# MLP up projection by Strassen's scheme: seven half-size products for a pair of chunks, with the down projection following pair by pair

## The reference, cut to what matters

```python
x = x + merged @ w_out[l]
h2 = rms_norm(x, norm2[l])
x = x + jnp.square(jax.nn.relu(h2 @ w_up[l])) @ w_down[l]     # w_up 1024 x 4096, w_down 4096 x 1024
return rms_norm(x, final_norm)
```

## Time and profile before

| what | us |
|---|---|
| median of three runs (2026.22, 2026.28, 2030.49) | 2026.28 |
| the profiled execution | 2030.5 |
| its span, first to last instruction | 2028.7 |
| PE busy | 1977.2 (97%) |
| DVE / ACT / POOL busy | 750.2 / 588.9 / 735.8 |
| granted TensorE clock, mean of the span | 0.993 |

### The profile page before, as it was taken

One profiled execution on the slowest core, in us unless ns is written; L12 is line 12 of the kernel. 1 busy time (PEld: TensorE's weight loads), 2 busy tenths in 40 slices (PEclk: granted clock), 3 DMA queues, 4 the chain that ended last, 5 costly groups with the idle time before them and its releaser, 6 DMA issues.

```text
span 2028.7 us, 28162 instructions
## 1 busy us (share of the span) xinstructions
PE 1977.2 (97%) x9984; PEld 1663.9 (82%) x9984; DVE 750.2 (37%) x1406; ACT 588.9 (29%) x1036; POOL 735.8 (36%) x633
## 2 busy tenths in 40 slices
PE   7999999999999999999999999999999999999998
PEld 6778887788888888888888887878888888888887
DVE  5535554667554544454421234321112112111222
ACT  5025544646444544455300011121011001101222
POOL 3442227623122212211344444434444444444441
PEclk9999999999999999999999999999999999999999
DMA  4311013331111011100111113111111111111112
GB/s 125 105 43 31 27 38 89 83 122 40 40 40 47 22 48 47 43 22 21 37 47 47 51 47 129 47 42 52 47 47 52 47 47 52 47 47 52 47 47 98
DMA packets 178293, 109.52 MB, mean 54 GB/s; under 512 B 11784, under 2 KB 171024, under 8 KB 178208
## 3 DMA queue, kind: packets, MB, share of 16 engines
q1 hardware_dynamic: 165984, 89.67, 15.6%
q10 hardware_dynamic: 12224, 18.70, 2.9%
HBM read 99.91 MB, written 11.59 MB: 55 GB/s over the span
## 4 chain that ended last, share of the span: by engine, by line
PE 89%; DVE 6%; issue 2%; ACT 2%; DMA 1%; SPq 0%; DVEq 0%; ACTq 0%
PE ps L582 23%; PE ps L583 23%; PE ps L584 23%; PE ps L702 6%; PE ps L691 3%; PE ps L677 2%; PE ps L672 1%; PE ps L624 1%; PE ps L626 1%; PE ps L625 1%; DVE tmp L1328 1%; DVE h_lo L1258 1%; DVE sumsq L1273 1%; PE ps L603 1%; PE ps L641 0%
## 5 line engine op out<-in xcount | busy, mean ns | idle before, releaser
L513 POOL TENSOR_TENSOR w_hi<-raw,ones 128x512 fp32r<-128x512 f32 x274 | 295.0, 1077 | 1207.9 <-PE ps L584 1192.1
L582 PE MATMUL ps<-h_hi,w_hi 128*128 128x512 f32 x1536 | 606.4, 395 | 11.8 <-DVE tmp L1328 3.4
L583 PE MATMUL ps<-h_lo,w_hi 128*128 128x512 f32 x1536 | 600.0, 391 | 0.0
L584 PE MATMUL ps<-h_hi,w_lo 128*128 128x512 f32 x1536 | 599.4, 390 | 0.0
L517 POOL TENSOR_TENSOR w_lo<-raw,w_hi 128x512 fp32r<-128x512 f32 x274 | 366.3, 1337 | 21.5
L582 PEld LDWEIGHTS ps<-h_hi,w_hi 128*128 128x128 f32 x1536 | 289.5, 188 | 69.6 <-DVE tmp L1328 5.9
L584 PEld LDWEIGHTS ps<-h_hi,w_lo 128*128 128x128 f32 x1536 | 288.9, 188 | 61.9
L583 PEld LDWEIGHTS ps<-h_lo,w_hi 128*128 128x128 f32 x1536 | 289.6, 189 | 54.5 <-issue 0.7
L582 PE MATMUL ps<-u_hi,w_hi 128*128 128x512 f32 x512 | 200.0, 391 | 2.7 <-DVE relu L1764 2.7
L584 PE MATMUL ps<-u_hi,w_lo 128*128 128x512 f32 x512 | 199.7, 390 | 0.0
L583 PE MATMUL ps<-u_lo,w_hi 128*128 128x512 f32 x512 | 199.6, 390 | 0.0
(11 more groups left out here) (232 smaller groups left out, 2378.9 us busy)
## 6 DMA issues: line engine op xcount, KB each, us to landing
raw<-in_w_in SPq DMA_DIRECT2D x116, 256.0 KB, 2.9
raw<-in_w_up SPq DMA_DIRECT2D x64, 256.0 KB, 2.7
raw<-in_w_down SPq DMA_DIRECT2D x64, 256.0 KB, 2.8
raw<-in_w_out SPq DMA_DIRECT2D x32, 256.0 KB, 2.8
x_in<-in_x SPq DMA_DIRECT2D x8, 512.0 KB, 7.7
raw_b<-in_w_out SPq DMA_DIRECT2D x16, 256.0 KB, 2.8
x_store<-X ACTq DMA_DIRECT2D x8, 512.0 KB, 2.8
bias_fox<-c_rows ACTq DMA_DIRECT2D x8, 512.0 KB, 4.5
```

The source lines that it names most:

```text
L513: pool.tensor_tensor(w_hi[:, half].rearrange("p k n -> p (k n)"), raw[:, half].rearrange("p k n -> p (k n)"), f32(ones[:, 0:1]).broadcast_ ...
L582: pe.matmul(o, w1, hi[:, k, c], start=first, stop=False)
L583: pe.matmul(o, w1, lo[:, k, c], start=False, stop=False)
L584: mm = pe.matmul(o, w2, hi[:, k, c], start=False, stop=last)
```

## The change

Two up chunks (256 hidden channels) become one pair; there are 16 pairs. In a pair the up weights are a 2x2 block matrix (two halves of k by two chunks), the activations another (two halves of k by two halves of the tokens). The four result blocks come from seven products P1 to P7 of half size, each four k tiles x one token half x three passes = 12 matmuls, 84 in all. Sums of activation blocks are made once for the stage: the operands b11, b21, b22, t1, t2, t3, t4, each with hi and lo part, [128, 4, 512]. Sums of weight blocks are made for each pair, by GpSimd: four additions or subtractions on 128x512 (`combine`) beside the seven splits. The down projection follows every pair: k over its 256 channels, eight output chunks of 12 matmuls (`down`), weights in four slots D0 to D3, two chunks each. Split weights go through four slots in the order of `weight_order`; a slot is filled again when TensorE is done with it. All loops over pairs are written out. OUT2 computes its rows in the order 0, 4, 1, 5, 2, 6, 3, 7.

Three PSUM banks and one more (A double, C, D) take the products. P1 is kept by ScalarE (`keep_first`) and P2 added on top in the bank; the partial sums are combined by VectorE in `r_t`.

```diff
+def weight_order():
+    order = [("P1", 0), ("P5", 0), ("P6", 0)]
+    for i in range(PAIRS_UP):
+        last = i + 1 == PAIRS_UP
+        if i:
+            order += [(f"D{j}", i - 1) for j in range(4)]
+        order += [("P2", i), ("P7", i)]
+        if not last:
+            order += [("P1", i + 1)]
+        order += [("P4", i), ("P3", i)]
+        if not last:
+            order += [("P6", i + 1), ("P5", i + 1)]
+    return order + [(f"D{j}", PAIRS_UP - 1) for j in range(4)]
...
+            def load_up(i):
+                if i >= 2:
+                    sp.wait_ge(w_made, W_AT["P3", i - 2] + 1)
+                elif i == 0:
+                    sp.wait_ge(merged, KT)
+                else:
+                    sp.wait_ge(mean_done, 5)
+                    sp.wait_ge(u_lo_made, 20)
...
+            def split_to_slot(op, src):
+                n = W_AT[op]
+                slot = n % W_SLOTS
+                if n >= W_SLOTS:
+                    name, i = W_ORDER[n - W_SLOTS]
+                    if name[0] == "P":
+                        pool.wait_ge(p_done, P_AT[name, i] + 1)
+                    else:
+                        pool.wait_ge(down_done, 8 * i + 2 * int(name[1]) + 2)
...
+                pool.tensor_tensor(hi, src, one, ALU.mult).then_inc(slot_hi_made, 1)
+                pool.wait_ge(slot_hi_made, n + 1)
+                pool.tensor_tensor(lo, src, f32(hi), ALU.subtract).then_inc(w_made, 1)
+            def combine(dst, a, b, op):
+                made.done(pool.tensor_tensor(dst, a, b, op))
+                made.wait()
+            def sums(i):
+                pool.wait_ge(up_2_loaded[i % 2], 16 * (i // 2 + 1))
+                pool.wait_ge(w_made, W_AT["P1", i] + 1)
+                if i == 0:
+                    pool.wait_ge(halves_done, 2 * G_MLP)
+                combine(sum_up[:], block(i, 2, 1), block(i, 2, 2), ALU.add)
+                combine(block(i, 2, 1), block(i, 2, 1), block(i, 1, 1), ALU.subtract)
+                combine(block(i, 1, 1), sum_up[:], block(i, 1, 1), ALU.subtract)
...
+            for i in range(PAIRS_UP):
+                for j in range(4 if i else 0):
+                    n = 4 * (i - 1) + j
+                    pool.wait_ge(down_loaded[n % 2], 16 * (n // 2 + 1))
+                    split_to_slot((f"D{j}", i - 1), down_raw[n % 2][:])
+                split_to_slot(("P2", i), block(i, 1, 2))
+                split_to_slot(("P7", i), block(i, 2, 1))
+                if i + 1 < PAIRS_UP:
+                    pool.wait_ge(up_1_loaded[(i + 1) % 2], 16 * ((i + 1) // 2 + 1))
+                    split_to_slot(("P1", i + 1), block(i + 1, 1, 1))
+                split_to_slot(("P4", i), block(i, 2, 2))
+                pool.wait_ge(w_made, W_AT["P2", i] + 1)
+                combine(block(i, 1, 2), block(i, 1, 2), block(i, 1, 1), ALU.subtract)
+                split_to_slot(("P3", i), block(i, 1, 2))
+                if i + 1 < PAIRS_UP:
+                    pool.wait_ge(w_made, W_AT["P5", i] + 1)
+                    sums(i + 1)
+                    split_to_slot(("P6", i + 1), block(i + 1, 1, 1))
+                    split_to_slot(("P5", i + 1), sum_up[:])
...
+            first_of_a(0)
+            first_of_c(0)
+            mean_square(4)
+            first_of_d(0)
+            for i in range(PAIRS_UP):
+                if i:
+                    down(i - 1)
+                pe.wait_ge(s1_made, i + 1)
+                product("P2", i, BANK_A[i % 2], first=False)
+                pe.wait_ge(d_read, 3 * i + 1)
+                product("P7", i, BANK_D, first=False)
+                if i == 0:
+                    spread_rms(4)
+                if i + 1 < PAIRS_UP:
+                    first_of_a(i + 1)
+                pe.wait_ge(d_read, 3 * i + 2)
+                product("P4", i, BANK_D, first=False)
+                pe.wait_ge(c_read, 2 * i + 1)
+                product("P3", i, BANK_C, first=False)
+                if i + 1 < PAIRS_UP:
+                    first_of_d(i + 1)
+                    first_of_c(i + 1)
+            down(PAIRS_UP - 1)
```

VectorE after it. The first pair, and with it the operands that are made late, then the loop over the other pairs and the end:

```diff
+            b22_rest(0)
+            b22_rest(1)
+            inverse_root(4)
+            keep_v(0)
+            t4_sum(0)
+            t4_sum(1)
+            t4_rest(0)
+            t4_sum(2)
+            t4_rest(1)
+            keep_u3(0)
+            t4_sum(3)
+            t4_rest(2)
+            t4_rest(3)
+            add_22(0)
+            b22_rest(2)
+            b22_rest(3)
...
+            for i in range(1, PAIRS_UP):
+                for q in range(8):
+                    add_down(i - 1, q)
+                dve.wait_ge(hid_ready, 4 * i)
+                relu_11(i)
+                keep_u3(i)
+                add_22(i)
+                relu_sum(1, N2, c_read, 2 * i + 1)
+                rest(4 * i, 0, N1)
+                add_21(i)
+                relu_sum(1, N1, d_read, 3 * i + 3)
+                rest(4 * i + 1, 1, N2)
+                add_12(i)
+                relu_sum(0, N2, c_read, 2 * i + 2)
+                rest(4 * i + 2, 1, N1)
+                rest(4 * i + 3, 0, N2)
+                if i + 1 < PAIRS_UP:
+                    keep_v(i + 1)
+            for k in range(KT):
+                add_down(PAIRS_UP - 1, k)
+                add_square(2, k)
```

More of the change, by code:

```diff
@@ L852, in _, with product @@
                 chunk(G_OUT2 + 2 * i + 1, 1)
[L853 to L860, removed]
-                    spread_rms(4)
[L862 to L868, removed]
+            def product(name, i, to, first=True):
+                n = W_AT[name, i]
+                hi, lo = slot_hi[n % W_SLOTS], slot_lo[n % W_SLOTS]
+                b_hi, b_lo = OPERAND[name]
+                pe.wait_ge(w_made, n + 1)
+                for k in range(4):
+                    if i == 0:
+                        if name == "P4":
+                            pe.wait_ge(t4_ready, k + 1)
+                        elif name == "P3":
+                            pe.wait_ge(b22_ready, k + 1)
+                        else:
+                            pe.wait_ge(u_lo_made, 5 * k + {"P1": 1, "P5": 2, "P2": 3, "P6": 4, "P7": 5}[name])
+                    o = bank(to)
+                    pe.matmul(o, hi[:, k], b_hi[:, k], start=first and k == 0, stop=False, skip_group_check=not first)
+                    pe.matmul(o, hi[:, k], b_lo[:, k], start=False, stop=False, skip_group_check=not first)
+                    mm = pe.matmul(o, lo[:, k], b_hi[:, k], start=False, stop=first and k == 3,
+                                   skip_group_check=not first)
+                mm.then_inc(p_done, 1)
@@ L932, in inverse_rms @@
                     return
+                if between is not None:
+                    between()
                 act.wait_ge(spread_done, n + 1)
@@ L1215, in _ @@
             act.wait_ge(halves_done, 2 * G_OUT2)
-            for k in range(KT):
[L1217 to L1233, removed]
@@ new lines, in _ @@
+            act.wait_ge(halves_done, 2 * G_MLP)
+            b22_top(0)
+            b22_top(1)
+            inverse_rms(4, (pairs_free, G_OUT2 + 2), between=late_operands)
+            for i in range(PAIRS_UP):
+                if i == 0:
+                    keep_first(1)
+                    hidden(0, 0, 1, N2)
+                    hidden(0, 1, 1, N1)
+                    hidden(0, 2, 0, N2)
+                    hidden(0, 3, 0, N1)
+                    continue
+                hidden(i, 4 * i, 0, N1)
+                hidden(i, 4 * i + 1, 1, N2)
+                if i + 1 < PAIRS_UP:
+                    keep_first(i + 1)
+                hidden(i, 4 * i + 2, 1, N1)
+                hidden(i, 4 * i + 3, 0, N2)
@@ new lines, in _ @@
+            t4_rest(0)
[8 more added lines that the diff above has]
+            b22_rest(3)
+            add_21(0)
+            add_12(0)
+            dve.wait_ge(rstd_ready, 3)
+            relu_sum(1, N2, c_read, 1)
+            relu_sum(1, N1, d_read, 3)
+            relu_sum(0, N2, c_read, 2)
+            relu_11(0)
+            rest(0, 1, N2)
+            rest(1, 1, N1)
```

345 lines of the change are left out of this document (285 added, 60 removed).

## The result

The changed kernel takes 2039.66 us (median of 4, 2039.1 to 2042.24) where the kernel before, run beside it, takes 2026.25 (median of 4, 2025.69 to 2030.49): ratio 1.0064, 95% interval 1.0047 to 1.0082. It is slower, by 13.4 us; 2040 was predicted. The profiled execution took 2039.33 with a span of 2037.5, against 2030.5 and 2028.7.

The account below looks back on a forecast made before the run. The prediction took TensorE's matmuls to bound the kernel. Its terms, -43.5 + 21 + 23.4 + 7.4 + 5.6 = +13.9 us, took the median from 2026.3 to 2040, own range 2026 to 2052, 8-in-10 range 2008 to 2057.

Parts of the forecast that it names:

- 192 matmuls fewer: Up projection on TensorE: 84 instead of 96 matmuls in each of 16 pairs, 43.5 us less.
- 14 steady pairs late: GpSimd's work from D3 to the next D0: turns exceed the slack by 1.5 us a pair, 21 us more.
- start, net: Stage start after OUT2: waits and clock loss of 27.4 us, less 4.0 lost there before, +23.4.
- last pair and end: Last pair's waits and clock, +7.4 us; last additions to X paced by VectorE's 3.5 us row, +5.6.
- The pace: TensorE's matmuls: 0.2267 us each was expected to hold, so 2.72 us a product.
- the mean turn: Steady pairs: each VectorE instruction with two SBUF inputs costs GpSimd 0.33 to 0.45 us, mean 0.39.
- the clock: Stage start: TensorE's clock drops after a long wait, 1.4 us lost at each of four waits, 5.6.
- The +2.5: Stage start: time added to `inverse_root`'s 4.0 us because GpSimd splits beside it; P7 then waits 2.7.
- A: Rival for the whole kernel: turns cost nothing because VectorE's instructions fall beside GpSimd's waits; 1999 us, chance 0.16.
- B: Rival for the steady pairs: the slack holds, the start is as forecast; 2019 us, chance 0.14.
- C: Rival for GpSimd's combines: additions on strided blocks take 1.62 us, 18 us more; 2058 us, chance 0.18.
- waits of about 0.5 at P6, P5 and D0: Sign in a steady pair: TensorE's waits named w_lo at these three places, about 0.5 us each.

Follow-up runs that it names:

- e4: Changed kernel with, in the last down part, each row's square added up after the next row's addition to X: 2039.4 us, ratio 1.0034 to the kernel before.
- e1: Changed kernel with one input in PSUM for all seven VectorE instructions of a pair that had two in SBUF: 2016.15 us, ratio 0.9930 to the kernel before.
- e3: Changed kernel with GpSimd's weight sums for the next pair made before P4's split, from pair 1 on: 2022.5 us, ratio 0.9962 to the kernel before.
- e5: Changed kernel with GpSimd making the first weight sum of every pair but the first twice: 2072.84 us, ratio 1.0212 to the kernel before.
- e8: e1 with the first weight sum of every pair but the first made twice: 2030.28 us, one run without an interval.
- e7: Changed kernel with the edits of e1, e3 and e4 plus the t4 sums held in PSUM: 2003.91 us, ratio 0.9879 to the kernel before.
- e2: Changed kernel with one PSUM input for only the three relu sums of a pair, the four `rest` unchanged: 2028.2 us, ratio 0.9992 to the kernel before.

## Why the prediction was right, term by term

The four terms each came out within 2.2 us of what was predicted:

| term | predicted | measured |
|---|---|---|
| 192 matmuls fewer | -43.5 | -43.5 (pace 0.2267) |
| 14 steady pairs late | +21 | +18.8 (1.34 each) |
| start, net | +23.4 | +22.5 |
| last pair and end | +13.0 | +12.9 |
| sum | +13.9 | +10.7 (milestones: +10.2) |

The medians of the runs are 13.4 apart, with an interval of 9.5 to 16.6 (the ratio's, times 2026.25). The 3 us between the two lie within the scatter of single executions, of which each trace is one: with e4's start and first pair the milestones give +12.5. And the kernel before came out at 2031.5 and 2030.64 in the later comparisons, for 2026.25 here. That 2040 met 2039.66 to 0.3 us is therefore luck; that the change costs some 10 to 13 us is not.

**The pace** held: products of 12 come 2.72 us apart, and e1's pair is 40.80, which is 180 x 0.2267.

**The steady pairs.** The mechanism is shown from both sides: without the turns (e1) and with the chain shortened but the turns kept (e3) the 1.34 us vanish; with one instruction more in the chain (e5) 1.30 are added, and in most rounds a half-clock stretch on top. The size was 1.5 for 1.34 because the mean turn was 0.36, not 0.39: five of seven fell on two-input instructions, at the low end of the range. Two of the seven lengthened instructions are D0's, where the prediction expected 1.04 and 1.29. The Trainium skill ("SBUF — State Buffer", section "SBUF: two separate sides") calls the shared port pair an exclusive lock and "not a bandwidth split". The rows agree: GpSimd's instructions are lengthened by 0.29 to 0.53, VectorE's by up to 1.1, each `rest` ends 0.54 to 0.56 behind the GpSimd instruction beside it, and nothing is lengthened once one input of each lies in PSUM (e1's groups).

**The start.** As excess over the pace, from matmul starts: P5 5.5 (predicted 5.8), P7 0.5 (2.7), P4 6.3 (5.3), its later k tiles and b22 2.9 (2.6), the first down part 5.5 (5.4), the clock 2.6 + 1.3 + 1.5 (5.6 in four equal parts). The mis-sized step is P7: `inverse_root` was costed at 6.5 us and took 4.9 (1318.19 to 1323.07). GpSimd was taken to split P2, P7 and P1 beside it without a pause; it stood idle for 2.01 us, waiting for the weights of the next pair's P1, and only one tiny instruction met it (1.16). That was the mildest case: in each of the eight traces of e1 to e8 GpSimd waits 1.5 to 1.8 us there, two of VectorE's instructions are lengthened, and P7 waits 1.0 to 1.3 us instead of 0.30. The +2.5 itself was a judgement: five times 0.90 less 0.18 would be 3.6. What P7 didn't wait, P4 waited instead, since `keep_u3` stands behind a chain of t4 that is VectorE's own: together 6.8 against 8.0. The clock behind P5's wait cost 2.6, not 1.4, because eleven starts in a row came 0.43 apart (granted clock 0.50 in its row; the earlier trace rows had 0.54, over fewer).

**The end.** The last pair was 5.9 late (38.51 - 32.64; predicted 6.0 without the clock), and the last addition 7.0 later than before (30.29 - 23.3; predicted 5.6 and 1.4 of clock). e4 shows the order on VectorE as the cause.

**The rivals.** A (turns cost nothing, 1999) fails on the rows of the steady round; its number is near e7's, for another reason. B (slack holds, 2019): the slack was there, 1.2, and 2.55 of turns were more; e3 is what B would have been, and came out at ratio 0.9962, 2018.5 of 2026.25. C (combines at 1.62) had the duration right for two of the four, for the wrong cause: alone a combine takes 1.29 (e1). What would be seen was listed as waits of about 0.5 at P6, P5 and D0; they are 0.41, 0.42 and 0.38 by the starts, but only P6's shows by name, at 0.25.

## What to carry to other kernels

Before work is taken off the bounding engine, walk the order of its feeder from the event that frees a buffer to the next use of it; an engine at 78% busy can be late by its order, and moving three instructions into an idle gap (e3) did as much for a pair as removing every collision (e1), though it left VectorE's chain no slack. Where GpSimd is on that path, give VectorE's instructions beside it one input in PSUM. Count the first and last rounds on their own: here they cost 35 us of the 43.5 gained, and the edits that turned +0.6% into -1.2% are a few lines each.

## What the runs showed of the hardware that I had not expected

- A single wait of 1.93 us in a dense stream was followed by the half clock (matmuls 0.43 apart seven times in a row, 1.2 us lost in the pair) in ten of thirteen rounds of e5; in three it was not, with the same wait. With waits of 0.6 once a pair (e8) the granted clock was 1.00 over the whole stretch.
- In the kernel after a turn costs 0.33 us on a two-input 128x512 instruction of GpSimd and 0.45 on a one-input one. These are no constants: e2 has 0.53 on an addition in place, and e3 0.45 on a two-input w_lo (1738 ns in the mean of 14) and 0.29 on a w_hi (1.33). VectorE's `rest` grows far more, from 0.68 to between 1.5 and 1.78.
- It is not only instructions with two SBUF inputs that are held: in e1, e2, e3, e5 and e7 a 128x8 `tensor_scalar` of `inverse_root`, with one SBUF input, took 1.15 or 1.16 us beside GpSimd, where the others took 0.17.
- GpSimd's additions on strided 128-wide blocks in place cost as much as on whole rows, 1.29.
